# A two-block transformer on one NeuronCore: the gathered token tile is selected first, its rows go into other buffers, and the one-hot operands are made in another way

## The reference, cut to what matters

```
q  = (hn @ w_query)                       # 8 heads x 2 halves x 128
sc = q . sub_keys                         # per token, 8 heads x 2 halves x 128 scores
v1, i1 = top_k(sc[half 0], 16);  v2, i2 = top_k(sc[half 1], 16)
top, pos = top_k(v1[:, None] + v2[None, :], 16)      # 16 of 256 candidates per head
idx  = i1 * 128 + i2 at pos;  gate = softmax(top)    # 8 x 16 = 128 slots per token
coef = gate * gelu(hn . expert_down[idx])            # expert tables: 16384 rows x 1024
out  = h + sum over slots of coef * expert_up[idx]
```

## Time and profile before

| | |
|---|---|
| three runs | 5107.29, 5112.29 (median), 5118.22 us |
| the profiled execution | 5117.36 us, its span 5115.4 us |
| PE busy, share of the span | 4215.2 us, 82% |
| DVE busy | 3292.2 us, 64% |
| ACT busy | 1985.2 us, 39% |
| POOL busy | 578.8 us, 11% |
| DMA, mean over the span | 206 GB/s |

### The profile page before, as it was taken

The page is one execution under the profiler, slowest core; times in us unless marked ns, Lnnn a source line. Parts: engine busy times, 40 slices in busy tenths (PEclk is TensorE's granted clock), DMA queues, the critical chain, the costliest instruction groups (busy, mean ns, idle before and its releaser), DMA issues. The chain is left out here.

```text
span 5115.4 us, 60334 instructions
## 1 busy us (share of the span) xinstructions
PE 4215.2 (82%) x23048; PEld 3354.7 (66%) x23048; DVE 3292.2 (64%) x4731; ACT 1985.2 (39%) x2053; POOL 578.8 (11%) x375
## 2 busy tenths in 40 slices
PE   6674559999999999994946596788789889988889
PEld 6473455566665566663736576588779889976667
DVE  2335738888888888883265443423249999777776
ACT  2212207766766667762222122222223333322222
POOL 0000000000000000000000000000000014566664
PEclk9886679999999999997966867899889999999999
DMA  2020019999999999991311102112245559999996
GB/s 84 18 67 21 33 43 362 369 359 373 371 356 370 362 357 374 370 354 45 98 35 46 40 1 84 50 58 89 65 144 164 191 188 368 390 336 329 330 322 230
DMA packets 486235, 1054.62 MB, mean 206 GB/s; under 512 B 22722, under 2 KB 189378, under 8 KB 473624
## 3 DMA queue, kind: packets, MB, share of 16 engines
q1 hardware_dynamic: 445736, 908.80, 50.0%
q0 software_dynamic: 40304, 143.16, 7.7%
HBM read 988.73 MB, written 63.17 MB: 206 GB/s over the span
## 5 line engine op out<-in xcount | busy, mean ns | idle before, releaser
L1247 DVE TENSOR_TENSOR ffn_low<-ffn_raw,ffn_high 128x2048 fp32r<-128x2048 f32 (+1 forms) x576 | 1190.0, 2110 | 245.7 <-ACT ffn_high L1200 245.4
L1200 ACT CAST ffn_high<-ffn_raw 128x2048 fp32r<-128x2048 f32 (+1 forms) x576 | 986.8, 1765 | 403.0 <-DMA ffn_raw<-in_w_gate 138.1
L2369 ACT CAST peer_high<-peer_raw 128x1024 fp32r<-128x1024 f32 x256 | 256.2, 1049 | 552.7 <-PE peer_ps L266 294.4
L2418 DVE TENSOR_TENSOR peer_low<-peer_raw,peer_high 128x1024 fp32r<-128x1024 f32 x256 | 313.2, 1267 | 96.2 <-ACT peer_high L2369 95.9
L264 PE MATMUL peer_ps<-peerbuf_hnT_high,peer_high 128*128 128x384 f32 x1024 | 355.5, 347 | 22.3 <-ACT peer_high L2369 19.6
L266 PE MATMUL peer_ps<-peerbuf_hnT_low,peer_high 128*128 128x384 f32 x1024 | 346.1, 338 | 0.0
L265 PE MATMUL peer_ps<-peerbuf_hnT_high,peer_low 128*128 128x384 f32 x1024 | 346.1, 338 | 0.0
L2352 PE MATMUL peer_ps<-peer_high,peerbuf_hnT_high 128*128 128x512 f32 x768 | 250.6, 409 | 85.7 <-DVE peerbuf_hnT_low L2423 81.8
L264 PE MATMUL ffn_gate_p<-ffn_high,ffn_x_high 128*66 128x512 f32 (+1 forms) x768 | 290.2, 378 | 13.7 <-DVE ffn_low L1247 13.5
L264 PE MATMUL ffn_down_p<-ffn_high,ffn_t_high 128*66 128x512 f32 x704 | 279.4, 397 | 14.5 <-DVE ffn_low L1247 14.5
L264 PE MATMUL ffn_up_p<-ffn_high,ffn_x_high 128*66 128x512 f32 (+1 forms) x768 | 288.7, 376 | 2.7 <-DVE ffn_low L1247 2.7
(11 more groups left out here) (565 smaller groups left out, 9783.5 us busy)
## 6 DMA issues: line engine op xcount, KB each, us to landing
ffn_raw<-in_w_gate SPq DMA_DIRECT2D x80, 2048.0 KB, 9.6
ffn_raw<-in_w_up SPq DMA_DIRECT2D x80, 2048.0 KB, 9.9
ffn_raw<-in_w_down SPq DMA_DIRECT2D x80, 2048.0 KB, 10.4
peer_raw<-in_peer_down_t SPq DMA_DIRECT2D x64, 1024.0 KB
peer_raw<-in_peer_up_t SPq DMA_DIRECT2D x64, 1024.0 KB
scratch_a<-peer_gelu SPq DMA_DIRECT2D x64, 384.0 KB
scratch_g<-peer_spread SPq DMA_DIRECT2D x24, 1024.0 KB, 9.3
peer_spread<-scratch_g SPq DMA_DIRECT2D x16, 1536.0 KB, 19.2
```

Of the source, the lines that this page charges most:

```text
L1200: act.copy(half_of(high, q, h), half_of(raw, q, h)).then_inc(high_done, 1)
L1247: dve.tensor_tensor(half_of(low, q, h), half_of(raw, q, h), half_of(high, q, h).bitcast(F32), ALU.subtract).then_inc(low_done, 1)
L2369: act.copy(high[:, q % 2, cols], raw[:, q % PR_RAW, cols]).then_inc(high_done, 1)
L2418: dve.tensor_tensor(low[:, q % 2, cols], raw[:, q % PR_RAW, cols], high[:, q % 2, cols].bitcast(F32), ALU.subtract).then_inc(low_done, 1)
```

## The change

1. The selection takes the token tiles in the order 3, 0, 1, 2 (`SEL_TILES`). Groups of a dense tile can start only when its own `finish` is done, now one place later. The dots may start once the first `finish` is done.
2. `ROW_RING` is 7: three tiles of `hn`, `h[:, NT]`, and `h[:, 0..2]` in place of the halves of `sc` and `cand`. The residual tiles `h[:, 0..2]` are stored to DRAM at the start (`h_dram`, 1536 KB) and loaded back after the last row is used.
3. The plan: budget 6.0 for 5.5, up to 3 groups a block after the selection, and 1 row a block while there is selection, 4 up to block 63, then 2, 2, 3 in turn. The gates of the gathered tile get a buffer of their own.
4. The first one-hot of a group's four tokens is made by one DVE comparison of 128x512. The second, times the gate, is made on GpSimd, four `tensor_scalar` of 128x128 a group, ahead of the block's other GpSimd work.
5. `g_dram` is `[G_LOADS, P, G_BATCHES, G_KEYS * G_BATCH]`: a load of a part is 12 KB contiguous in each partition; a store of a batch is 16 pieces of 512 bytes in each partition.

```diff
-ROW_RING = 8
+ROW_RING = 7
+SEL_TILES = [DENSE] + list(range(DENSE))
@@ peer_plan
-    before = {"dot": ("sel", DENSE, last), ...}
+    before = {"dot": ("finish", 0), ...}
+    def group_ready(b):
+        return groups and placed_by(b - 2, ("finish", groups[0][0] + 1))
-        budget, many = 5.5, 0
+        budget, many = 6.0, 0
-        while not sel and groups and many < 2 and placed_by(b - 2, ("finish", groups[0][0])):
+        while not sel and group_ready(b) and many < 3:
-        while rows and taken < (3 if many or b >= PAIRS else 4):
+        most = 1 if sel else 4 if b < PAIRS else 2 + (b % 3 == 0)
+        while rows and taken < most:
@@ peer_experts
-        rows = [hn[:, 0, :], hn[:, 1, :], hn[:, 2, :], h[:, NT, :], sc[:, 0:D], sc[:, D:2 * D],
-                cand_rows[:, 0:D], cand_rows[:, D:2 * D]]
+        rows = [hn[:, i, :] for i in range(DENSE)] + [h[:, NT, :]] + [h[:, i, :] for i in range(DENSE)]
@@ sync
-                sp.dma_start(sc[:, :], score_dram[0]).then_inc(select.sc_in, 16)
+                sp.dma_start(sc[:, :], score_dram[SEL_TILES[0]]).then_inc(select.sc_in, 16)
+                sp.dma_start(h_dram.rearrange("t p d -> p t d"), h[:, 0:DENSE, :]).then_inc(h_out, 16)
-                            sp.dma_start(g_dram[:, n, :, :].rearrange("p k t -> p (k t)"),
-                                         staged[:, n % 2, :, :].rearrange("p k t -> p (k t)")
+                            sp.dma_start(g_dram[:, :, n, :].rearrange("g p c -> p g c"),
+                                         staged[:, n % 2, :, :].rearrange("p (g k) t -> p g (k t)", g=G_LOADS)
-                            sp.dma_start(g_tile[:, g % 2, :, :, :], g_dram[:, :, g * G_KEYS:(g + 1) * G_KEYS, :]
+                            sp.dma_start(g_tile[:, g % 2, :, :, :].rearrange("p n k t -> p n (k t)"), g_dram[g]
                 sp.wait_ge(row_used, n_rows)
+                sp.dma_start(h[:, 0:DENSE, :], h_dram.rearrange("t p d -> p t d")).then_inc(h_back, 16)
@@ gpsimd
-                        pool.wait_ge(select.selected, NT)
+                        pool.wait_ge(select.selected, 1)
+                    elif n == DENSE + 1:
+                        pool.wait_ge(h_out, 16)
                 for q in range(PEER_BLOCKS):
+                    for task in plan[q]:
+                        if task[0] == "g":
+                            i, n = task[1], group_no[task]
+                            pool.wait_ge(turn_taken, i + 1)
+                            if n >= AB_RING:
+                                pool.wait_ge(group_done, n - AB_RING + 1)
+                            for t in range(G_TOK):
+                                col = task[2] * G_TOK + t
+                                pool.tensor_scalar(onehot[:, n % AB_RING, 1, t, :], select.iota[:, :],
+                                                   turned[:, i % 2, 1, col:col + 1], turned[:, i % 2, 2, col:col + 1],
+                                                   ALU.is_equal, ALU.mult).then_inc(gated, 1)
@@ vector
-                            for t in range(G_TOK):
-                                col = task[2] * G_TOK + t
-                                first, second, gate = (turned[:, i % 2, w, col:col + 1] for w in range(3))
-                                dve.tensor_scalar(onehot[:, n % AB_RING, 0, t, :], select.iota[:, :], first, None,
-                                                  ALU.is_equal).then_inc(onehot_done, 1)
-                                dve.tensor_scalar(onehot[:, n % AB_RING, 1, t, :], select.iota[:, :], second, gate,
-                                                  ALU.is_equal, ALU.mult).then_inc(onehot_done, 1)
+                            first = turned[:, i % 2, 0, task[2] * G_TOK:(task[2] + 1) * G_TOK]
+                            dve.tensor_tensor(onehot[:, n % AB_RING, 0, :, :],
+                                              select.iota[:, :].unsqueeze(1).broadcast_to([P, G_TOK, PEER_KEYS]),
+                                              first.unsqueeze(2).broadcast_to([P, G_TOK, PEER_KEYS]),
+                                              ALU.is_equal).then_inc(onehot_done, 1)
+                dve.wait_ge(h_back, 16)
                 for t in range(DENSE):
                     dve.wait_ge(tile_summed, t + 1)
@@ second_block
-    g_dram = nc.dram_tensor("scratch_g", [P, G_BATCHES, PEER_KEYS, G_BATCH], F32).ap()
+    g_dram = nc.dram_tensor("scratch_g", [G_LOADS, P, G_BATCHES, G_KEYS * G_BATCH], F32).ap()
+    hd_dram = nc.dram_tensor("scratch_hd", [DENSE, P, D], F32).ap()
```

More of the change, by code:

```diff
@@ L1979, in peer_plan @@
     rows = [("dot", n) for n in range(PEER_SLOTS)] + [("coef", 0)] + [("acc", n) for n in range(PEER_SLOTS)]
-    before = {"dot": ("sel", DENSE, last), "coef": ("dot", PEER_SLOTS - 1), "acc": ("coef", 0)}
+    before = {"dot": ("finish", 0), "coef": ("dot", PEER_SLOTS - 1), "acc": ("coef", 0)}
     at = {}
@@ L2000, in peer_plan @@
             budget -= SEL_COST[n]
-            if groups and many < 3 and placed_by(b - 2, ("finish", groups[0][0])):
+            if group_ready(b) and many < 3:
                 place(b, ("g", *groups.pop(0)))
                 many += 1
-        while not sel and groups and many < 2 and placed_by(b - 2, ("finish", groups[0][0])):
+        while not sel and group_ready(b) and many < 3:
             place(b, ("g", *groups.pop(0)))
@@ L2108, in piece @@
         else:
-            if i == DENSE:
+            if i == 0:
                 for a, b in ((0, 1), (1, 0)):
@@ L2123, in finish @@
         dve.wait_ge(self.exp_ready, i + 1)
-        if i >= 2:
-            dve.wait_ge(turned, i - 1)
+        gates = self.row_gates[:, :] if i == 0 else self.gates[:, i % 2, :]
+        if i >= 3:
+            dve.wait_ge(turned, i - 2)
         t = self.top[:, i % 2, :, :]
@@ L2128, in finish, with peer_experts @@
         order(dve.reciprocal(self.total[:, :], self.total[:, :]))
-        order(dve.tensor_tensor(self.gates[:, i % 2, :].rearrange("p (h t) -> p h t", h=H), t,
+        order(dve.tensor_tensor(gates.rearrange("p (h t) -> p h t", h=H), t,
                                 self.total[:, :].unsqueeze(2).broadcast_to([P, H, T]), ALU.mult))
         dve.sem_inc(self.finished, 1)
-def peer_experts(nc, io, hn, hnT, h, ident, score_dram, a_dram, g_dram, out):
+def peer_experts(nc, io, hn, hnT, h, ident, score_dram, a_dram, g_dram, h_dram, out):
     plan, at = peer_plan()
@@ L2185, in peer_experts @@
             st.sem(x) for x in ("product_done", "c_high_done", "c_low_done", "tile_summed", "added", "stored"))
-        idx_done, row_used, dots_gelu, coef_done = (
-            st.sem(x) for x in ("idx_done", "row_used", "dots_gelu", "coef_done"))
+        idx_done, row_used, dots_gelu, coef_done, h_out, h_back, gated = (
+            st.sem(x) for x in ("idx_done", "row_used", "dots_gelu", "coef_done", "h_out", "h_back", "gated"))
         row_in = [st.sem(f"row_in{s}") for s in range(ROW_RING)]
@@ L2301, in turn @@
                                              select.picked[:, 1, :, :].rearrange("p h t -> p (h t)"),
-                                             select.gates[:, i % 2, :])):
+                                             select.gates[:, (i + 1) % 2, :])):
                         pe.transpose(ps[:, 6, w * P:(w + 1) * P], src, ident[:, :]).then_inc(turn_done, 1)
                 def spread_group(n):
-                    pe.wait_ge(onehot_done, 2 * G_TOK * (n + 1))
+                    pe.wait_ge(onehot_done, n + 1)
+                    pe.wait_ge(gated, G_TOK * (n + 1))
                     if n >= 2:
@@ L2314, in _ @@
                 for q in range(PAIRS):
-                    tasks = [t for t in plan[q] if t[0] in ("finish", "g") and t[1] < DENSE]
+                    tasks = [t for t in plan[q] if t[0] == "g" or (t[0] == "finish" and t[1] >= 1)]
                     pe.wait_ge(high_done, 2 * (q + 1))
@@ L2332, in _ @@
                                 if kind == "finish":
-                                    turn(i)
+                                    turn(i - 1)
                                 else:
@@ L2379, in _ @@
                     for task in (plan[q - 1] if 1 <= q <= PEER_BLOCKS else ()):
-                        if task[0] == "finish" and task[1] < DENSE:
-                            i = task[1]
+                        if task[0] == "finish" and task[1] >= 1:
+                            i = task[1] - 1
                             act.wait_ge(turn_done, 3 * (i + 1))
@@ L2450, in _ @@
                             dve.wait_ge(dots_gelu, 1)
-                            dve.tensor_tensor(coef[:, :], dots[:, :], select.gates[:, DENSE % 2, :], ALU.mult
+                            dve.tensor_tensor(coef[:, :], dots[:, :], select.row_gates[:, :], ALU.mult
                                               ).then_inc(coef_done, 1)
```

15 lines of the change are left out of this document (8 added, 7 removed).

## The result

The changed kernel takes 5221.9 us (median of 4 runs, 5219.9 to 5235.7) against 5115.26 us (4 runs) for the one before: ratio 1.0214, 95% interval 1.0197 to 1.0230. It is 2.1% slower, where 5004 us was forecast. The profiled execution took 5219.9 us with a span of 5218.2, and in it the 102.8 us over the span of before lie as follows, with the same cuts as in the earlier trace rows.

The account below looks back on a forecast made before the run. Bounds taken: PE, then DVE in blocks 9 to 35, PE in 36 to 63, and PE's floor plus about 120 us of DMA stalls in pass 2. Terms -42 + 25 - 95 + 4 = -108 from 5112 gave 5004 us, range 4968 to 5070.

Parts of the forecast that it names:

- the price in the part on GpSimd's comparisons: Each gated one-hot comparison on GpSimd was taken at 0.35 us, between bounds of 0.2 and 0.8.
- That hides, barely: Blocks 36 to 54: 12 comparisons and four gathers cost POOL 10.8 us a block against PE's 11.02.
- the allowance of 10: Blocks 36 to 63: 0.5 us a block added for DMA excess in the 19 blocks with groups, 10 us.
- 0.4 us a block on DVE: Blocks 18 to 35: one collision a block in which a GpSimd comparison holds DVE, 7 us in all.
- Rival (d): Dense stretch: GpSimd comparison much dearer than the cast; gain gone at 0.89 us, 5138 us at 1.0; chance 0.06.
- rival (c): Blocks 21 on: the port lock holds DVE for each whole comparison, 57 to 95 us more, 5061 to 5099; chance 0.07.
- Blocks 0 to 35: The selection stretch, bound mostly by DVE, was to fall from 407.4 to 365 us, -42.
- pass 2: Pass 2 and the end were to fall from 654.2 to 559 us, -95, with G loads in long runs.
- rival (a): Pass 2 stays bound by transfers at the old rate whatever the pieces, 9.2 us a block, 5040 us; chance 0.17.
- 512-byte stores hold SP: A sign that would show the forecast wrong: G stores in 512-byte pieces hold SP's queue.
- Rival (b): Dense stretch bound by transfers, 512-byte stores at 160 GB/s: +38 us on the forecast, 5042 us; chance 0.12.
- Rival (e): Whole kernel: nothing arrives, as the pieces of G and the rows only trade places, about 5110 us; chance 0.03.

Follow-up runs that it names:

- run 5: Changed kernel with a group's four gated one-hots on GpSimd in four forms (scalars from a tensor, constants, one comparison, plain copy), part of the result left out: 5162.2 us.
- run 1: Changed kernel with the gated one-hot back on DVE, four small comparisons a group, all else as changed: 5052.3 us, ratio 0.9873.
- run 6: Changed kernel in which DVE reads only the first element of each gathered down row in place of the dot, part of the result left out: 5133.9 us.
- run 2: Kernel before the change with the contiguous layout of G in DRAM alone: 5068.2 us, ratio 0.9910.
- run 3: Changed kernel with the gated one-hot back on DVE (run 1) and the old layout of G: 5082.6 us, ratio 0.9931.
- run 10: On run 1: every second of the first 39 groups' gates on GpSimd, three rows a block up to block 54, then four to 63: 5023.1 us, ratio 0.9818.

## Why the prediction was wrong

**The step that failed** is the price in the part on GpSimd's comparisons: "I take 0.35, near the cast of 0.397, since two operations are done on half as many elements". It measured 0.78 alone and 1.31 on average. Scaling a conversion by elements left out three things that run 5 prices one by one: that it compares, that there is a second operation, and that its scalars come from SBUF. A plain copy of 128x128, 0.29 us, is itself dearer than half of the cast. The upper bound, 0.8, was right for a comparison alone, but it was taken at 0.35 because the nearest row looked near; the two rows stood a factor of two apart and neither was a comparison. With it fell "That hides, barely": 4.2 us in the text are 16.1 in the trace, and POOL's block of 10.8 against PE's 11.02 is one of 21.0. The price alone does not make the kernel slower, though: by the prediction's own sum 0.78 us gives blocks of 12 x 0.78 + 6.6 = 15.96 us, 84 us more than forecast (19 x 4.94 less the allowance of 10), 5088 in all and still under the 5112 of before. The second term that failed is the hold on POOL, put at nothing: the text counted 0.4 us a block on DVE, and in the block shown 6.8 us were spent on POOL.

**Rival (d) is what happened**, at a chance of 0.06, but for half its reason: it has a comparison dearer than the cast, not one that is held, and its break-even, c = 0.89, lies above what a comparison takes alone. With the measured 1.31 its formula gives blocks of 12 x 1.31 + 6.6 = 22.3 us, and 19 of them with nine of 8.32 are 499 us, where 486 were measured. That it comes so near is in part luck: the 19 blocks took 383 us and not 424 (four gathers take 4.95 us and not 6.6), and the nine behind them 103 and not 75, with the block of 17.9 us and the rows' backlog in them. The 6.8 us spent held in a block are 129 us in 19 blocks; without them the kernel would take about 5093 us, a little under before. That is an estimate from one block (the mean comparison of the whole dense stretch, 1.345 us, gives the same 6.8); no run had the comparisons unhindered beside the same DVE work.

**The lock was charged to the wrong engine.** I counted 0.4 us a block on DVE, and rival (c) its whole length, from the 4.01 us of the earlier trace rows, where one long POOL multiplication held DVE. Here the small comparisons lose: the three under DVE's burst take 9.1 us where they need 2.3, while DVE's own operations all but keep their times: in the dense stretch a dot has a mean of 1.26 us and a longest of 1.45, where run 1, with no comparison on POOL, has 1.21 and 1.22. Not every DVE operation holds POOL. The 47 comparisons beside which DVE ran only the selection's searches and reductions took 0.78 to 0.80 us, and the 200 beside which it ran nothing 0.78 to 0.81; the 90 beside two-input operations alone took 2.65 on average. The Trainium skill ("SBUF — State Buffer", "SBUF: two separate sides") has the port pair of the two engines as an exclusive lock for a whole instruction; the trace agrees that one waits for the other, and run 6 that two-input operations of DVE do it. Who loses is less clear. DVE's next operation is ready when its last ends, and POOL's comparison, already waiting, still does not get in between; but POOL's comparisons come back to back too. So this is a reading of these timelines and no cause that is shown: no run tried DVE with gaps between. One sum of that part is also off: 39 groups of four comparisons of 0.35 us are 55 us, not 57.

**Blocks 0 to 35** gave 10 us where 42 were forecast. The first two tiles came out as worked (72.7 and 84.7 us). The third and fourth took 111.4 and 128.9 where the DVE sums were 92.6 and 102.6: 56 and 100 comparisons, and POOL busy 87.28 and 127.24 us. With the gate back on DVE (run 1) they cost the same 398 through DVE instead. Half on each gives 380 and, on before, all on POOL 373. In run 5, whose comparisons are cheaper, the stretch took 364, so the forecast of 365 hung, at least in part, on the same price.

**Right**: pass 2 (-104 against -95), so rival (a) is out; half of its gain, though, is from the rows moved ahead and not from the pieces, as runs 2 and 3 show. The start (+4.6 against +4). The issue behind a part, no longer held. The sign "512-byte stores hold SP" came true in single cases (run 2, and once in the changed kernel), beside the point of the loss. The wide comparison, 0.6 us on DVE from its start to the next one's. Rival (b), 512-byte stores at 160 GB/s, is out as a bound on the dense stretch by run 2 and by run 10's PE-bound stretch at 364 GB/s. Rival (e) is out. On G's layout the trace had already spoken against the rule of the Trainium skill ("DMA: Bandwidth & Descriptors", "Specifications") that transfers from 512 bytes up run at line rate, by which regrouping wins nothing: loads in 512-byte pieces did cost (runs 2 and 3, with the reservation on addresses made there), stores in such pieces did not in run 2.

## What to carry to other kernels

Work moved to an idle engine is priced by an operation of the same kind there or by both ends of the bound, and if the verdict turns between the ends, as here at 0.89 us, the dear end gets a real chance. An engine idle on the average (POOL 11% of the span) can bind in the stretch where the moved work lands: add up its queue for that stretch, with the time for which a bursting DVE holds it. Split such work by stage: the gate on GpSimd was worth 18 us in the selection, at half of the groups, and cost 170 us when all of it also shared blocks with gathers.

## What the runs showed of the hardware

- GpSimd on 128x128 f32: copy 0.29 us, one comparison with a constant 0.53, with a second operation 0.64, with both scalars from SBUF 0.78. On DVE four of the last kind take 1.0 us.
- The same GpSimd instruction took 1.3 us on average over the changed kernel and up to 4.6. Beside two-input operations of DVE alone it took 2.65 on average, beside DVE's searches and reductions 0.78 to 0.80. A plain copy took up to 2.0. DVE's dots lost 0.05 us on average.
- Loads in 3072 pieces of 512 bytes held the next issue 7 to 16 us, and that layout cost 36 to 45 us over pass 2. Stores in 2048 pieces of 512 bytes held the next issue in some cases, up to 10 us, and cost nothing that shows in run 2.
- With PE busy 361 of 486 us its granted clock averaged 0.82 in the changed kernel's blocks 36 to 63; with the gate back on DVE it was 0.99. PE's waits alone don't give the clock: in run 6 PE was busy 231 of 321 us, no larger a share, and had 0.98 (the row below).

```profile
4188.00:4509.00 321.00, 230.86 (x1354) 209.59 (x1354) 86.81 (x171) 84.09 (x131) 298.07 (x297) 0.98 0.80 255
```
